# Two-block forward pass on one core: one strip goes through device memory instead of through TensorE, another is sent earlier, one weight split waits a piece

## The reference, cut to what matters

```
h  = x + stick_breaking(rms_norm(x, norm_mix))            # w_qkv, w_o: 2048 wide, 256 tokens
h  = h + relu(rms_norm(h, norm_mlp) @ mlp_w1)**2 @ mlp_w2 # 2048 -> 8192 -> 2048
x2 = rms_norm(h, final_norm)
z  = rms_norm(x2, pre_mix_g) @ w_in                       # second block: q, k, v, u
m  = concat(chunked_attention(q, k, v), pool(u)) @ w_o
x2 = x2 + rms_norm(m, post_mix_g)
up = causal_dwconv(rms_norm(x2, pre_ffn_g) @ w_up)        # 2048 -> 11264
y  = (gelu(up[:5632]) * up[5632:]) @ w_down
out = x2 + rms_norm(y, post_ffn_g)
```

## Time and profile before

| | |
|---|---|
| median of 3 runs | 2122.08 us (2122.01 to 2123.68) |
| the profiled execution | 2123.21 us, span 2121.5 us |
| granted TensorE clock, mean | 0.999 |
| PE busy | 2112.6 us, 100% of the span |
| DVE, ACT, POOL busy | 1255.2, 1051.7, 190.1 us |
| DMA | 194 GB/s, 60.5% of the 16 engines' span on the main queue |

### The profile page before, as it was taken

How to read it: one execution, slowest core, us unless ns; L and a number is a source line. 1 busy time by engine, 2 the same in 40 slices (tenths; PEclk the granted TensorE clock), 3 DMA queues, 4 the chain that set the end, 5 groups by cost and what they waited for, 6 DMA issues and landing times.

```text
span 2121.5 us, 26812 instructions
## 1 busy us (share of the span) xinstructions
PE 2112.6 (100%) x11014; PEld 1812.9 (85%) x11014; DVE 1255.2 (59%) x1337; ACT 1051.7 (50%) x1224; POOL 190.1 (9%) x90
## 2 busy tenths in 40 slices
PE   9999999999999999999999999999999999999998
PEld 8888888888888888888888888888888888888887
DVE  6555656656455555465667755576666644666565
ACT  6654555544334443344555645465455433455543
POOL 3000000000000000000004000002222100222210
PEclk9999999999999999999999999999999999999999
DMA  8565557665666666665676656655655666556663
GB/s 288 166 209 174 179 169 231 221 197 174 209 195 184 196 209 194 182 195 193 219 237 189 187 171 196 192 183 174 193 191 181 212 195 189 182 176 203 202 208 120
DMA packets 218923, 411.98 MB, mean 194 GB/s; under 512 B 13360, under 2 KB 22704, under 8 KB 218288
## 3 DMA queue, kind: packets, MB, share of 16 engines
q1 hardware_dynamic: 217936, 405.77, 60.5%
q10 hardware_dynamic: 864, 4.49, 0.6%
HBM read 403.92 MB, written 6.29 MB: 193 GB/s over the span
## 4 chain that ended last, share of the span: by engine, by line
PE 98%; DMA 1%; DVE 0%; ACT 0%; issue 0%; SPq 0%; DVEq 0%
PE ps L1491 98%; DMA xT<-in_x_dram 0%; DMA E<-passed_rows 0%; PE ps L1494 0%; DMA passed_rows<-xN 0%; DVE aHL L1248 0%; DVE xN L1258 0%; DVE T L1237 0%; SPq L858 0%; DVE Wl L1141 0%; ACT aHL L944 0%; DVE aHL L1241 0%; SPq L863 0%; ACT T L1070 0%; DVE Wl L1137 0%
## 5 line engine op out<-in xcount | busy, mean ns | idle before, releaser
L1141 DVE TENSOR_TENSOR Wl<-raw,Wh 128x1024 fp32r<-128x1024 f32 x743 | 911.4, 1246 | 648.3 <-ACT Wh L920 647.6
L1491 PE MATMUL ps<-aHL,Wh 128*128 128x512 f32 x3336 | 1159.1, 392 | 1.6 <-DVE Wl L1137 1.0
L920 ACT ACTIVATE Wh<-raw 128x1024 fp32r<-128x1024 f32 x743 | 767.4, 1054 | 583.3 <-PE ps L1491 580.7
L1491 PE MATMUL ps<-aHL,Wl 128*128 128x256 f32 x3328 | 930.1, 280 | 0.0
L1491 PEld LDWEIGHTS ps<-aHL,Wh 128*128 128x128 f32 x3336 | 623.9, 187 | 140.7 <-issue 1.1
L1491 PEld LDWEIGHTS ps<-aHL,Wl 128*128 128x128 f32 x3328 | 628.3, 189 | 0.5
L1491 PE MATMUL ps<-Wh,hid 128*128 128x512 f32 x1728 | 532.6, 389 | 0.0
L1491 PEld LDWEIGHTS ps<-Wh,hid 128*128 128x128 f32 x1728 | 324.3, 188 | 67.4
L1491 PE MATMUL ps<-Wl,hid 128*128 128x512 f32 x864 | 336.2, 389 | 0.0
L1491 PEld LDWEIGHTS ps<-Wl,hid 128*128 128x128 f32 x864 | 162.2, 188 | 33.6
L1491 PE MATMUL ps<-Wh,oHL 128*128 128x512 f32 x512 | 158.8, 390 | 0.0
(11 more groups left out here) (177 smaller groups left out, 796.2 us busy)
## 6 DMA issues: line engine op xcount, KB each, us to landing
raw<-in_mlp_w_dram SPq DMA_DIRECT2D x256, 512.0 KB, 4.2
raw<-in_w_up_dram SPq DMA_DIRECT2D x176, 512.0 KB, 3.7
raw<-in_sb_w_qkv_dram SPq DMA_DIRECT2D x93, 512.0 KB, 4.8
raw<-in_w_down_dram SPq DMA_DIRECT2D x88, 512.0 KB, 4.2
raw<-in_w_in_dram SPq DMA_DIRECT2D x64, 512.0 KB, 4.6
raw<-in_sb_w_o_dram SPq DMA_DIRECT2D x32, 512.0 KB, 5.3
raw<-in_w_o_dram SPq DMA_DIRECT2D x32, 512.0 KB, 4.3
passed_rows<-xN SPq DMA_DIRECT2D x16, 256.0 KB, 4.3
```

The source lines that it names most:

```text
L920: e.activation(Wh[:, i % NW, :], rawv[:, i % NRAW, :], ACT.Copy).then_inc(st["hi"][0], 1)
L1141: e.tensor_tensor(Wl[:, i % NW, :], rawv[:, i % NRAW, :], Wh[:, i % NW, :].bitcast(F32), ALU.subtract).then_inc(st["lo"][0], 1)
L1491: return e.matmul(o, l, r, start=start, stop=stop, skip_group_check=True)
```

## The change

Four edits, all in the planner, and one in the preparation of the weights.

1. Place A: strip 3 no longer goes through `turn` (which is deleted) but through `move_rows`, and its factors (`gained`) are applied at once, not one piece later. The rows of `w_in_2` and of its gain are permuted for all four strips.
2. The load of the biases and what follows it are put off by six pieces.
3. Place B: the rows of strip 3 are added and sent to device memory right away, ahead of the work of strip 1; before, this was done a piece later, behind it. With it `turn_blocks` comes a piece earlier too.
4. At the early piece B1, one split fewer is emitted; the next piece emits two.

```diff
-    def turn(n, gain_name, need):
-
-        s = side_set()
-        turned = [done("rows_turned") for i in range(3)]
-        hi = [done("tile_hi") for j in range(4)]
-        lo = [done("tile_lo") for j in range(4)]
-        step("turn", n=n, set=s, gain=gain_name, tiles=(0, 1, 2, 3), need=[*need, ident, *free[f"set{s}"]], added=None,
-             turned=turned, hi=hi, lo=lo)
-        free[f"set{s}"] = [lo[3]]
-        tile_hl[4 * n:4 * n + 4] = lo
-
@@ -287,13 +276,13 @@
                     row_squares(s4, g, gained=True)
-                    if s4 < 3:
-                        move_rows(s4, "pre2", g)
-                    else:
-                        later(2, lambda: turn(s4, "pre2", g))
-                later(1, gained)
+                    move_rows(s4, "pre2", g)
+                if s4 < 3:
+                    later(1, gained)
+                else:
+                    gained()
             if more:
-                more(s, k[1])
+                later(6, lambda: more(s, k[1]))
@@ -498,11 +487,11 @@
             step("keep_last", set=s, row=st["mixed_row"], kept=kept[1])
+            add_rows(3)
+            move_rows(3, "ffn", added[3] * 2)
 
             def second_tiles():
                 tiles(1)
-                add_rows(3)
-                move_rows(3, "ffn", added[3] * 2)
                 add_rows(2)
             later(1, second_tiles)
             later(3, lambda: tiles(2))
@@ -678,7 +667,7 @@
-        while n_split <= (i + LEAD if i > 2 else i + 1):
+        while n_split <= (i + (LEAD - 1 if q["early"] else LEAD) if i > 2 else i + 1):
@@ -1693,7 +1682,7 @@
-_MOVED = {"mlp_w1": slice(0, 4), "norm_mlp": slice(0, 4), "w_in_2": slice(0, 3), "pre_mix_g_2": slice(0, 3),
+_MOVED = {"mlp_w1": slice(0, 4), "norm_mlp": slice(0, 4), "w_in_2": slice(0, 4), "pre_mix_g_2": slice(0, 4),
```

## The result

The changed kernel takes 2128.73 us (median of 7 runs, 2127.57 to 2134.80). The kernel before, on the same chip, takes 2122.40 us (7 runs, 2122.00 to 2123.68). The ratio is 1.0032, with a 95% interval of 1.0023 to 1.0041: slower by 6.3 us. The forecast was 2125.4 us, with a range of 2123.9 to 2128.4. The time lies 0.3 us above the range, on the side of the rival in which the clock falls.

A forecast was written before the change was run, and what follows sets the result against it. PE, busy 2112.6 us of the 2121.5 us span, was taken as the bound. As worked out (chance 0.50), -0.1 us at A and +3.4 at B make +3.3, so 2122.08 + 3.3 = 2125.4 us, range 2123.9 to 2128.4.

The forecast's parts named there:

- the rival in which the clock falls: At B: PE's clock halves behind the stall, costing 1.8 us more, so 2127.2 us; chance 0.33.
- the wait at B7: At place B: PE's wait for strip 3's low halves before B7 goes, winning 0.45 us.
- Place A, -0.87: At place A: removing the eight PE matmuls that transpose strip 3 wins 0.87 us.
- The stall of 0.8 us: At place A: PE waits 0.8 us at the spread for DVE's diagonal of the norms, bounds none to 3.7.
- Where the strip lands at A: At A: strip 3's reads start at 1098.9, its block transposition at 1103.7; the diagonal is ready 10.1 us after that.
- The stall of 3.8 us at B: Before B5: PE waits 3.8 us for strip 2's low halves, until t + 4.4, t being strip 3's transposition start, 1394.75.
- The biases at nothing: Loading the biases' 1 MB later costs nothing; a clash with the added DMAs would show as a late transposition start.
- The held split at nothing, its cover 0.8 us: At B: the held split costs nothing; strip 1's low halves start 0.25 us later, within 0.8 us of cover before B3.
- Both reads slow: Rival: strip 3's reads are late at both places, A +2.9 and B +4.6, giving 2129.6 us; chance 0.10.
- no stall in B: Rival: strip 3's transposition starts by 1390.9, so B5 waits for nothing, giving 2120.8 us; chance 0.05.
- (1) to (4) and (6): No transposes at A; PE waits at the spread and before B5, not at B7, nor for weights anywhere.
- Sign (5): Granted clock behind B's stall: 1.00 for the forecast, 0.5 for the rival in which the clock falls.

The follow-up runs named there:

- experiment 4: Changed kernel with 14 matmuls on ones, results unused, put into the stall between B4 and B5; 2126.77 us, ratio 1.0016.
- experiment 1: Kernel before with only the changed place A (strip 3 without transposes, gain at once) and the later biases; 2123.55 us, ratio 1.0004.
- experiment 7: Kernel before with the changed place A, the later biases and the chain of the norms' factors three pieces earlier; 2121.70 us, ratio 0.9995.
- experiment 8: Kernel before with the changed place A and later biases, but strip 3's gain applied a piece later again; 2128.19 us, ratio 1.0024.
- experiment 9: Kernel before with only the biases six pieces later and one split held back at the early piece; 2122.39 us, ratio 1.0000.
- place B alone: Kernel before with only strip 3 added and sent earlier at B and the held split; 2129.38 us, ratio 1.0032.
- experiment 11: Changed kernel with strip 2's work ahead of strip 3's transposition at B, the factors' chain earlier, and biases loaded at once; 2124.34 us, ratio 1.0007.
- experiment 10: Kernel before with strip 3 sent early at B, strip 2's work ahead of strip 3's transposition, no held split; 2122.91 us, ratio 1.0001.
- experiment 3: Changed kernel with strip 2's work put ahead of strip 3's block transposition at B; 2123.39 us, ratio 1.0001.

## Why the prediction was wrong

The step that failed is the choice between the forecast as worked out, 0.50, and "the clock falls in B's stall", 0.33. The clock fell in all three profiles with the whole stall, of 3.1, 3.2 and 4.7 us, and in the one with 1.9 us of idle time behind 1.3 us of ones; with the stall filled (experiment 4) it did not. The argument against it, that the half level stands only where PE had run 1 us out of more than 4 and that B's stall has full work on both sides, was wrong: full work on both sides did not hold the clock. The loss of the clock was priced at 1.8 us from matmuls on ones at either level; the runs gave 1.2 to 2.2 us by pairs, 1.8 between two profiles and 2.4 between two medians. Its price was right, and its case should have been the forecast: 2127.2 us, 1.5 below the median.

For the other 1.5 us the profiles show two terms that the sum had wrong. It took 0.45 us off for the wait at B7, read from one profile, which experiments 1, 7, 8 and 9 don't have with place B's strip 3 as before. And it took what a wait does to the pairs behind it at nothing. They ran in the slower rhythm, 1.4 us more up to the next transposes, in five of the eight profiles in which PE waits at the spread or at A7, and in none of the six in which it waits at neither. An estimate from the changed kernel's first profile, 0.6 for A up to the spread, 3.4 for the stall and 1.45 for the clock, is 5.5 us in the faster rhythm and 6.9 in the slower; the median lies between, at 6.3. How often each rhythm comes is not known, so this split is a reading, not a proof.

Point by point:

- *Place A, -0.87.* Right: no matmul of L1483 is left there. *The stall of 0.8 us* was 1.0 and 0.4 us in the two profiles of the changed kernel, 1.2 in experiment 1, its place and releaser right. The whole of A up to the spread cost 0.6, 0.0 and 0.8 us there, where the forecast had -0.1; by the medians, with what follows it, +0.7, within the noise of a median.
- *Where the strip lands at A.* Forecast 3.3 us from write to read and 4.8 to the transposition; 3.7 and 4.9 measured. The diagonal was ready 10.1 us behind that, as forecast.
- *The stall of 3.8 us at B*, within 3.0 to 5.1: 3.1 to 3.2 in the two profiles of the changed kernel (3.4 for the weight loads), 4.7 in place B alone. It is t + 4.4 in the first, to 0.01 us, as worked out: 1394.17 and 1398.57. What was off was t, by the read's 4.2 us against the 4.8 taken. The wait at B7 went, but it was not there to be won, as said above. That the stall was too large by 0.4 to 0.7 us hid a part of what the sum lacked: a piece of luck.
- *The biases at nothing.* Right as an edit by itself (experiment 9), and right that a clash "shows as a late t"; but the working did not see that edit 1 needs edit 2. Without it the reads of strip 3 started 4.3 us later behind its writes (experiment 11).
- *The held split at nothing, its cover 0.8 us.* The cover without it was too small by 0.25 us (experiment 10). The split's place was a price paid for the addition, and the forecast had it as an idle extra.
- *Both reads slow*, and *no stall in B*: neither came. The second needed t 3 us earlier; the real way to no stall was another order, which experiment 3 has.

The signs to look for, (1) to (4) and (6), all came as written. Sign (5) decided for the rival.

By the differences over before the parts are: A +0.7 (1), the stall at B +3.4 (4 less 3), the clock +2.4 (the changed kernel less 4), which is 6.5 against 6.3. The last two are differences along one chain of kernels and sum up by themselves; only the 0.7 of A against the 0.5 of experiment 3 is a check.

## What to carry to other kernels

When work is moved earlier on an engine that runs in order, ask what it now stands in front of: an instruction that waits for a DMA makes everything behind it wait too, so put what the bottleneck needs first ahead of it, even if both come due together. Price a stall of TensorE like these as the stall and the slower matmuls behind it: the clock fell behind 3.1, 3.2 and 4.7 us, behind 1.9 us with ones ahead of it, and not behind 1.2 or 1.45 us (experiments 1 and 11) or where ones filled it. A transfer that only has slack, like the biases here, can cost a tight one beside it its cover; test such edits together with the one that they stand next to, not only alone. And before a wait in a profile is booked as something to win, look for it in a second profile: the one at B7 was a slow read.

## What was not expected of the hardware

- Pairs of products at a granted clock of 1.00 and without a wait took 0.347 us in some stretches and 0.353 in others. At place A the rhythm changed at the transposes, at the spread or at a wait and then held for some 90 us. That is 1.4 us over 562 matmuls, more than the 0.87 us that edit 1 was made for.
- The clock fell to its lower level behind only 1.9 us without a matmul, and not at once: 1.2 us after the products had begun again (first profile of the changed kernel 1.15 us, the late gain in A 1.25 us). In the second profile of the changed kernel and in place B alone it was low from the first pair.
- A 1 MB load issued 0.6 us behind a write to device memory put the read that waits for that write off from 3.9 to 8.2 us.
- Reads of the same 0.5 MB took 4.1 to 5.8 us from issue to the transposition in these profiles, with the same order of instructions. That scatter alone moves the stall by more than the 0.87 us that the change could win.
